# Reading the delta rule's key norms from the diagonal of k·k

## The reference, cut to what matters

```
def _l2norm(x):
    return x * lax.rsqrt(jnp.sum(x * x, axis=-1, keepdims=True) + 1e-6)
...
    q = _l2norm(q) * HEAD_DIM ** -0.5
    k = _l2norm(k)
...
        kk = jnp.einsum('bhid,bhjd->bhij', kc, kc)
        lower = eye + jnp.where(strict, bc[..., :, None] * decay * kk, 0.0)
        rhs = bc[..., None] * vc - (bc * eg)[..., None] * jnp.einsum('bhcd,bhde->bhce', kc, s)
        u = lax.linalg.triangular_solve(lower, rhs, left_side=True, lower=True, unit_diagonal=True)
```

## Time and profile before

| what | value |
|---|---|
| three runs, median (lowest to highest) | 1653.81 us (1653.74 to 1655.29) |
| the profiled execution, its own time | 1657.26 us |
| its span in the trace | 1655.6 us |
| mean granted TensorE clock of the span | 0.996 of full |
| PE busy | 1632.9 us, 99% of the span |
| DVE, ACT, POOL busy | 1050.5, 617.3, 237.2 us |
| PE in the chain that ended last | 93% |

### The profile page before, as it was taken

One profiled execution on the slowest core, in us unless ns is written; L12 is line 12 of the kernel. 1 busy time (PEld: TensorE's weight loads), 2 busy tenths in 40 slices (PEclk: granted clock), 3 DMA queues, 4 the chain that ended last, 5 costly groups with the idle time before them and its releaser, 6 DMA issues.

```text
span 1655.6 us, 30927 instructions
## 1 busy us (share of the span) xinstructions
PE 1632.9 (99%) x12899; PEld 1585.7 (96%) x12899; DVE 1050.5 (63%) x1716; ACT 617.3 (37%) x786; POOL 237.2 (14%) x370
## 2 busy tenths in 40 slices
PE   7999999999999999999999999999999999999997
PEld 7999989988998998999999999999999999999997
DVE  5676688656544455676666666666666666666665
ACT  6444323332343343643333333333333333333334
POOL 1121342123213022210000010101010101010004
PEclk9999999999999999999999999999999999999999
DMA  8453355344857467444544444444445444445442
GB/s 239 131 153 111 110 145 162 102 117 142 255 184 244 140 209 232 135 146 149 158 148 153 153 148 147 151 153 149 145 152 153 147 148 150 154 140 155 151 153 84
DMA packets 231243, 256.64 MB, mean 155 GB/s; under 512 B 9444, under 2 KB 220966, under 8 KB 231104
## 3 DMA queue, kind: packets, MB, share of 16 engines
q1 hardware_dynamic: 217856, 220.10, 43.2%
q0 software_dynamic: 10560, 33.29, 6.4%
q10 hardware_dynamic: 2688, 1.27, 0.3%
HBM read 243.50 MB, written 12.69 MB: 155 GB/s over the span
## 4 chain that ended last, share of the span: by engine, by line
PE 93%; DVE 3%; DMA 1%; issue 1%; ACT 1%; POOL 0%; SPq 0%; DVEq 0%; POOLq 0%; ACTq 0%
PE ps_proj L1774 22%; PE ps_proj L1775 21%; PE ps_proj L1776 21%; PE ps_small L1774 6%; PE ps_small L1776 6%; PE ps_small L1775 6%; PE ps_small L1816 2%; DMA w_raw<-in_w_in_dram 1%; PE ps_small L2048 0%; PE ps_small L1958 0%; PE ps_small L2136 0%; DVE w_lo L1173 0%; PE ps_small L1948 0%; PE ps_small L2154 0%; DMA state_s<-in_state_gdn_dram 0%
## 5 line engine op out<-in xcount | busy, mean ns | idle before, releaser
L1774 PE MATMUL ps_proj<-x_hi,w_hi 128*128 128x320 f32 x2432 | 766.2, 315 | 1.5 <-DVE x_lo L1290 1.0
L1776 PE MATMUL ps_proj<-x_hi,w_lo 128*128 128x320 f32 x2432 | 752.3, 309 | 0.0
L1775 PE MATMUL ps_proj<-x_lo,w_hi 128*128 128x320 f32 x2432 | 752.3, 309 | 0.0
L821 ACT ACTIVATE w_hi<-w_raw 128x1024 fp32r<-128x1024 f32 x408 | 432.1, 1059 | 741.4 <-PE ps_proj L1776 546.2
L1173 DVE TENSOR_TENSOR w_lo<-w_raw,w_hi 128x1024 fp32r<-128x1024 f32 x408 | 498.1, 1223 | 302.4 <-ACT w_hi L821 302.0
L1774 PEld LDWEIGHTS ps_proj<-x_hi,w_hi 128*128 128x128 f32 x2432 | 457.3, 188 | 15.0 <-issue 9.9
L1775 PEld LDWEIGHTS ps_proj<-x_lo,w_hi 128*128 128x128 f32 x2432 | 457.9, 188 | 0.2
L1776 PEld LDWEIGHTS ps_proj<-x_hi,w_lo 128*128 128x128 f32 x2432 | 457.4, 188 | 0.0
L1774 PE MATMUL ps_small<-hid_hi,w_hi 128*128 128x320 f32 x704 | 218.0, 310 | 0.0
L1776 PE MATMUL ps_small<-hid_hi,w_lo 128*128 128x320 f32 x704 | 217.6, 309 | 0.0
L1775 PE MATMUL ps_small<-hid_lo,w_hi 128*128 128x320 f32 x704 | 217.5, 309 | 0.0
(11 more groups left out here) (351 smaller groups left out, 1217.0 us busy)
## 6 DMA issues: line engine op xcount, KB each, us to landing
w_raw<-in_w_up_dram SPq DMA_DIRECT2D x176, 512.0 KB, 3.5
w_raw<-in_w_in_dram SPq DMA_DIRECT2D x112, 512.0 KB, 3.8
w_raw<-in_w_down_dram SPq DMA_DIRECT2D x88, 512.0 KB, 3.5
w_raw<-in_w_out_dram SPq DMA_DIRECT2D x32, 512.0 KB, 4.1
k_pages<-in_cache_k_dram POOLq DMA_DIRECT2D x32, 256.0 KB, 3.4
v_pages<-in_cache_v_dram POOLq DMA_DIRECT2D x32, 256.0 KB, 4.3
state_s<-in_state_gdn_dram POOLq DMA_DIRECT2D x10, 512.0 KB, 5.5
out_ss_dram<-state_s POOLq DMA_DIRECT2D x8, 512.0 KB, 4.5
```

What stands on the lines that cost most here:

```text
L821: act.activation(whi[:, slot], raw[:, slot], ACT.Copy).then_inc(hi_done, 1)
L1774: pe.matmul(o, hi, rhs_hi[:, k0 + kk_, :], start=first and kk_ == 0, stop=False)
L1775: pe.matmul(o, hi, rhs_lo[:, k0 + kk_, :], start=False, stop=False)
L1776: ins = pe.matmul(o, lo, rhs_hi[:, k0 + kk_, :], start=False, stop=last and kk_ == CQ - 1)
```

## The change

The keys are no longer squared in `qs`, and `nr` keeps the four products of the squared queries alone. A new DVE step `kn`, behind PE's `kk`, multiplies b1 by the identity, sums each row, adds epsilon and takes over the small operations of `ss`. `rn` and `dc`, which need its results, move behind it, ahead of DVE's `kk`. The planner's table gets a length for `kn` (28) and `dc` (8), and a shorter one for `nr` (3 for 5).

```
--- before.py
+++ after.py
@@ -180,12 +180,12 @@
 
 
 def decay_steps(k):
-    return [("V", "gt", *k), ("P", "cg", *k), ("V", "dm", *k), ("A", "de", *k), ("V", "dc", *k)]
+    return [("V", "gt", *k), ("P", "cg", *k), ("V", "dm", *k), ("A", "de", *k)]
 
 
 def gdn_steps(g):
     decay = decay_steps((g, 0))
-    s = decay[:1] + [("A", "qs", g, 0), ("P", "nr", g, 0), ("V", "ss", g, 0), ("G", "rn", g, 0)] + decay[1:]
+    s = decay[:1] + [("A", "qs", g, 0), ("P", "nr", g, 0), ("V", "ss", g, 0)] + decay[1:]
     tail = []
     for u in (0, 1, 2):
         k, nxt = (g, u), (g, u + 1)
@@ -194,21 +194,20 @@
         s += [("P", "kk", *k)]
         if u < 2:
             s += [("A", "qs", *nxt)]
-        s += [("V", "kk", *k), ("G", "mk", *k, 2)]
+        s += [("V", "kn", *k), ("G", "rn", *k), ("V", "dc", *k), ("V", "kk", *k), ("G", "mk", *k, 2)]
         if u == 1:
             s += [("G", "si", g, 0), ("G", "si", g, 1)]
         if u == 2:
             s += [("G", "mk", *k, 4), ("G", "zm", g), ("G", "si", g, 2)]
         s += [("V", "kq", *k)]
         if u < 2:
-            s += [("P", "nr", *nxt), ("V", "ss", *nxt), ("G", "rn", *nxt)]
+            s += [("P", "nr", *nxt), ("V", "ss", *nxt)]
         s += tail[:1] + [("P", "tk", *k), ("V", "tk", *k)]
         beside = {2: [("P", "tv", *k), ("V", "bv", *k)], 4: []}
         if u < 2:
             decay = decay_steps(nxt)
             beside[4] += decay[:1]
             beside[8] = decay[1:4]
-            beside[16] = decay[4:]
         if u == 0:
             beside[4] = beside.pop(2) + beside[4]
         if u == 1:
@@ -299,11 +298,11 @@
 
 
 LENGTH = {
-    "P": {"nr": 5, "cg": 5, "kk": 12, "tk": 6, "tv": 6, "pl": 6, "dx": 6, "ph": 4, "dh": 6, "pf": 5, "df": 5, "u": 9,
+    "P": {"nr": 3, "cg": 5, "kk": 12, "tk": 6, "tv": 6, "pl": 6, "dx": 6, "ph": 4, "dh": 6, "pf": 5, "df": 5, "u": 9,
           "os": 20, "ot": 6, "gs": 7,
           "ks": 9, "us": 12, "sh": 11, "kv": 12, "S": 11, "O": 12, "kt": 10, "hb": 6, "SS": 6, "PT": 4, "PV": 16, "OT": 2, "ab": 76},
     "A": {"sc2": 25, "sc5": 24, "ab": 10, "qs": 10, "pl": 8, "o": 10, "oq": 0, "kv": 16, "E": 14, "SE": 9, "gs": 10, "kt": 8, "PT": 9, "fp": 22},
-    "V": {"sc1": 11, "sc3": 50, "sc4": 15, "ss": 0, "gt": 0, "dm": 10, "dc": 0, "kk": 20, "kq": 9, "tk": 0, "bv": 0,
+    "V": {"sc1": 11, "sc3": 50, "sc4": 15, "ss": 0, "gt": 0, "dm": 10, "dc": 8, "kn": 28, "kk": 20, "kq": 9, "tk": 0, "bv": 0,
           "o2": 0, "oz": 0, "dx": 10, "dh": 4, "df": 4, "dg": 6, "ks": 8, "st": 0, "oc": 10, "o1": 0, "um": 8, "us": 28, "hk": 8,
           "S": 16, "N": 9, "SS": 15, "SN": 7, "kt": 8, "hb": 12, "qz": 3},
     "G": {"rn": 0, "or": 0, "so": 0, "si": 0, "s2": 0, "gs": 0, "zm": 0, "zv": 0, "kv": 0, "pk": 0, "pv": 0, "hk": 110, "mk": 9, "xd": 0, "qz": 0},
@@ -899,8 +898,7 @@
                         after(act, "P", "cg", g, u - 1)
                     else:
                         after(act, *before_group(g))
-                    act.activation(qn[:, :, 0:n], reg[g][:, 0:4, c0:c0 + n], ACT.Square)
-                    finish(act.activation(kb[:, :, 0:n], reg[g][:, 4:8, c0:c0 + n], ACT.Square))
+                    finish(act.activation(qn[:, :, 0:n], reg[g][:, 0:4, c0:c0 + n], ACT.Square))
                 elif name == "de":
                     n = unit(k[1])[0]
                     after(act, "V", "dm", *k)
@@ -1330,10 +1328,17 @@
                     n, _ = unit(u)
                     after(dve, "P", "nr", g, u)
                     bank, rows = (b3 if u else b0), out_rows(u)
+                    finish(dve.tensor_scalar(small[rows, cols["eq"][0] + 4 * u:cols["eq"][0] + 4 * u + 4], bank[rows, 0:4],
+                                             EPS, EPS * P, ALU.add, ALU.mult))
+                elif name == "kn":
+                    g, u = k
+                    n, _ = unit(u)
+                    after(dve, "P", "kk", g, u)
+                    own = at_[0:n, :, 0:n]
                     cc, kx = of_unit("cc", n, u), of_unit("kx", n, u)
-                    dve.tensor_scalar(small[rows, cols["eq"][0] + 4 * u:cols["eq"][0] + 4 * u + 4], bank[rows, 0:4],
-                                      EPS, EPS * P, ALU.add, ALU.mult)
-                    chain(dve.tensor_scalar(kx, bank[0:n, 4:8], EPS, None, ALU.add))
+                    chain(tt(own, heads(b1[0:n], n), over_heads(C("ident", n, n), 4), ALU.mult))
+                    chain(dve.tensor_reduce(kx, own, AX.X, ALU.add))
+                    chain(dve.tensor_scalar(kx, kx, EPS, None, ALU.add))
                     chain(dve.reciprocal(cc, kx))
                     chain(tt(cc, cc, per_head("beta", n, u, g), ALU.mult))
                     finish(tt(of_unit("kc", n, u), cc, per_head("kd", n, u, g), ALU.mult))
@@ -1892,8 +1897,7 @@
                         after(pe, *(("V", "dm", g, 0) if u == 1 else ("V", "st", g, 0)))
                     bank, rows = (b3 if u else b0), out_rows(u)
                     for h in range(4):
-                        pe.matmul(bank[rows, h:h + 1], qn[:, h, 0:n], C("ones", P, 1), start=True, stop=True)
-                        ins = pe.matmul(bank[0:n, 4 + h:5 + h], kb[:, h, 0:n], C("ones", P, 1), start=True, stop=True)
+                        ins = pe.matmul(bank[rows, h:h + 1], qn[:, h, 0:n], C("ones", P, 1), start=True, stop=True)
                     finish(ins)
                 elif name in ("tk", "tv"):
                     g, u = k
@@ -2325,7 +2329,7 @@
                 elif name == "rn":
                     u = k[1]
                     n = unit(u)[0]
-                    after(pool, "V", "ss", *k)
+                    after(pool, "V", "kn", *k)
                     finish(pool.tensor_tensor(of_unit("kr", n, u), of_unit("kx", n, u), sm("hf", n), ALU.pow))
                 elif name == "mk":
                     g, u, l = k
```

## The result

The changed kernel is slower, by little but measurably: 1659.86 us median of 16 runs (1656.16 to 1662.36) against 1655.55 us for the kernel before in the same comparison (16 runs, 1653.33 to 1658.98). The ratio is 1.0025, 95% interval [1.0018, 1.0032]. I had forecast 1652.6 us and no change.

A forecast was written before the change was run, and what follows sets the result against it. PE, busy 99% of the span, was taken to set the end. From 1657.26 us, -3.6 -1.35 +1.9 +3.1 and clock -1.3 gave 1656.0 profiled, less 3.45 for the median: 1652.6 us, 8 in 10 within 1648 to 1656.5.

The forecast's parts named there:

- The product removed, -3.6: `nr` on PE: four products fewer save 0.88 us in each 128-token unit, 0.1 in both sample units; 3.6 us off.
- The idle at `pl`, -1.35: PE's wait for POOL's mask at `pl` of (0,2) goes, as `pl` stands one chunk farther from `kk`: -1.35 us.
- `kn`, 2.05 and 1.44 us: DVE's new step takes 2.05 us on 128 tokens, 1.44 on 64; covered in 128-token units, costed at nothing.
- The wait before `sh`, 1.9: `sh` of (0,2): PE waits 1.9 us for DVE's `oz`, partly at chunk 43 for `w_lo`; bounds 0 to 3.1.
- The wait at `ot`, 3.1: `ot` of (0,2): PE waits 3.1 us for DVE's `o2`, behind one more `w_lo` and two more taps; 0 to 4.5.
- The clock, -1.3: Half-level clock drops near `nr`: one fewer, as shorter `nr` should make them rarer; -1.3 us, between +1.3 and -2.6.
- Rival (c): Slower: DVE sets the pace, chunks 40 to 51; waits reach 7.6 us, one drop more adds 1.3; 1657.8 us, chance 0.13.

The follow-up runs named there:

- e3: The kernel before without the squares of k and their products, key norms read from those of q, so the output differs: 1651.93 us, ratio 0.9980.
- e1: The changed kernel with the planner's old lengths (nr 5, dc 0, kn 0), PE's steps back at or near their old places: 1669.16 us, ratio 1.0082.
- e7: The changed kernel with ACT's silu of the convolution issued behind the chunk's own steps: ratio to the kernel before 1.0001.
- e4: The changed kernel with the convolution's taps on chunks 48 and 49 cut to 8 of 344 columns: 1654.33 us, ratio to the kernel before 0.9991.
- e6: The changed kernel with `ot` later, by raising the planner's length for `us` from 28 to 34: ratio to the kernel before 1.0005.
- e12: Control: the kernel before with only ACT's silu issued behind the chunk's steps: ratio 0.9998.
- e8: The changed kernel with both `ot` later (`us` 34) and ACT's silu behind the chunk's steps: 1653.97 us, ratio to the kernel before 0.9988.
- e5: The kernel before with five extra multiplications by 1.0 on DVE ahead of `o2` of (0,2), to put in a rest at `ot`: ratio 1.0020.
- e11: The changed kernel with the silu behind the chunk's steps, `kn` length 20 for 28 and `us` 32 for 28: ratio to the kernel before 1.0000.
- e2: The kernel before, computation unchanged, with planner lengths that put PE's steps exactly at the changed kernel's places: ratio 1.0019.
- e9: The changed kernel with `nr`, `cg` and `kk` of (1,0) two chunks later: median 1659.07 us, ratio to the kernel before 1.0008.
- e10: The changed kernel with the silu behind the chunk's steps, `kn` length 24 for 28 and `us` 32 for 28: ratio to the kernel before 0.9993.

## Why the prediction was wrong

- **The product removed, -3.6.** Right. From its start to that of PE's next step, `nr` at full clock takes 0.80 us in a unit of 128 tokens (287.19 to 287.99 in the changed kernel), where it took 1.70, so four units give 3.6; in a sample unit it takes 0.56 where it took 0.57, so k's products were free there. e3 has 1.5 us left after its waits and, for a mean clock 0.0012 above the runs beside it, some 1.6 more by the price worked out below; it came out 3.3 us faster.
- **The idle at `pl`, -1.35.** Right, gone.
- **`kn`, 2.05 and 1.44 us.** 2.14 and 1.56. That it is covered in units of 128 tokens was right, and e1 shows what comes out without it: 13.4 us of waits, with the reservations there.
- **The wait before `sh`, 1.9.** It was 2.7, at `w_lo` (0.6) and `dx` (2.1). DVE's lag was sized right (1.8 in e7); that ACT's silu stood ahead of `pl`, and would hand the lag on to PE, I had not looked for.
- **The wait at `ot`, 3.1.** It was 2.8. With `inv`'s 0.5, which I had not seen, new waits are 6.0 us for 5.0.
- **The clock, -1.3.** This is the step that failed. "I count one drop fewer", on the ground that shorter `nr` steps make drops rarer. That ground is right alone (e3). But the same passage had the other side, that a rest at `ot` invites a drop, and let it widen the range without any weight in the sum. The trace has 6.9 us more at half level in the mixer, 13.7 for 6.8. At half level PE starts 9 to 11 matmuls in 2 us and not 16, and e4 puts 10.2 us of it at 4.2, so this costs some 2.8 us where I had counted a gain of 1.3. The runs agree in sign: the mean clock of the changed kernel's 16 is 0.9954, 0.0016 below the 95 of before, which over 1655 us is 1655 x 0.0016 / 0.5 = 5.3 us more at half level, some 2.2 us of time. This mean also takes in the stretch at the end of the span (4.0 us in this trace, 5.3 before, 10.0 in e6, 9.2 in e12), most of it behind PE's last product, so it measures the mixer only roughly.

Trace against trace the sum closes to half a microsecond. The profiled execution took 2.9 us longer (1660.15 for 1657.26). Off went 3.6 of products and 1.3 of idle at `pl`; on came 6.0 of new waits and 2.8 of clock; the waits for the first loads were 0.5 shorter. That makes +3.4. PE's busy time says the same: -3.6 + 2.8 = -0.8, and it fell by 0.9.

The forecast for a profiled execution, 1656.0, was thus 4.1 us too low: 4.1 for the clock and 1.0 for the waits, less the 0.5 at the start and 0.5 that is not accounted for. The other 3.1 of the miss of 7.3 us, 1659.86 for 1652.6, are of the step to a median. I took off 3.45, the distance of one trace from the median of three runs. Over 16 runs each, the profiled executions stood 1.7 us (before) and 0.3 us (after) above the medians: the three runs had come out low. Rival (c) named the mechanism, DVE's lag with a clock drop at `ot`, but gave it a chance of 0.13, as it was tied to waits at their upper bounds. Waits near the tally were enough, with 2.8 us of clock where (c) had 1.3.

The rest at `ot` is not the whole of it. e6 and e7 each undo one of two things, and e8 both. Moving `ot` takes 0.0020 off the ratio (e6 against the changed kernel) or 0.0013 (e8 against e7), though the waits fall by only 0.5 us net. Moving the silu takes off 0.0024 (e7) or 0.0017 (e8 against e6), for 0.9 us of waits. So 2 to 4 us of time hang on less than 1 us of waits in each place, and the half level in the mixer goes the same way: 13.7 us in the changed kernel, 3.4 in e6, 10.2 in e7, none in e8, one trace each. Each of the four ratios is known to about 0.0009, so the smaller two differences are barely clear of noise. It looks as if the waits at chunk 43, where ACT's silu stood in the way, cost through the clock too; that is argued from these numbers and not shown by itself.

The Trainium skill's page "TensorE: Matmul & The Clock Gate", section "Why this matters for your kernels", warns against idle gaps of TensorE between bursts, longer ones than any rest in the mixer here. I had set it aside, as the clock had fallen with PE never idle. The runs bear out both sides: e5 put one rest of 2.4 us into a kernel that was never idle there, and the clock fell 0.8 us behind it; e3 halved the one-column products, with somewhat more short waits, and two drops went. But a rest need not bring a drop: in e11 one of 2.9 us at `sh`, to 220.88, had none behind it until 263.7.

What stays open is why the drop behind a rest lasted 10.2 us in the changed kernel, e2 and e7, 6.8 in e9, and 3.4 in e5 and in e11. `nr` inside it is not settled as the cause: e9 speaks against. Nor does one profile stand for all runs of a kernel, and every length above is from one profile; e2's twelve lie in two groups (1654.6 to 1657.6 at clocks of 0.996 to 0.998, 1660.5 to 1664.0 at 0.993 and 0.994).

## What to carry to other kernels

When a step moves past others, list what it passes on every engine's queue, also on those that it only hands through: here ACT's silu turned DVE's lag into a wait of PE. On an engine that is busy 99%, price a new rest at more than its length (e6 to e8), and give a change of the clock a sign only after both the work removed and the rests added are weighed. A planner's length that covers a chain also moves all that comes after; the cure was not a shorter length (e10, e11) but a later reader of what the lagging engine makes, with ACT's hand-through out of the way (e8), and it brought the kernel to 0.9988, hardly below the one before.
